# Latent attention in layer 0: where TensorE makes the queries, who copies the turned keys, and when the low parts of w_out0a are cut

## What is computed

```
z, xbc, dt_raw, q_a, kv_a, k_pe = split_cols(h @ w_in, L0_SIZES)
...
y = ssd_chunked(xs, dt, a, b, c)
y = y + d_skip * xs
y_ssd = rmsnorm(y * silu(z), ssm_norm_g)
q = rmsnorm(q_a, q_a_norm_g) @ w_q_b                 # 8 heads of 64 + 32, the 32 rotated by position
kv = rmsnorm(kv_a, kv_a_norm_g) @ w_kv_b             # 8 heads of 64 (key) + 64 (value)
k = concat(kv[..., :64], broadcast(apply_rope(k_pe)))  # 32 rotated key rows, the same for all heads
o_mla = causal_block_attention(q, k, kv[..., 64:], 96 ** -0.5)
return concat([y_ssd, o_mla]) @ w_out
```

## Time and profile before

| | us |
|---|---|
| median of 3 executions | 2051.86 |
| lowest, highest | 2048.86, 2054.71 |
| the profiled execution | 2055.55 |
| its span | 2053.8 |
| TensorE busy | 1928.1 (94%) |
| VectorE busy | 1379.4 (67%) |
| ScalarE busy | 985.5 (48%) |
| GpSimd busy | 262.5 (13%) |
| mean granted TensorE clock | 0.977 of full |

### The profile page before, as it was taken

One profiled execution on the slowest core, in us unless ns is written; L12 is line 12 of the kernel. 1 busy time (PEld: TensorE's weight loads), 2 busy tenths in 40 slices (PEclk: granted clock), 3 DMA queues, 4 the chain that ended last, 5 costly groups with the idle time before them and its releaser, 6 DMA issues.

```text
span 2053.8 us, 33496 instructions
## 1 busy us (share of the span) xinstructions
PE 1928.1 (94%) x13340; PEld 1775.8 (86%) x13340; DVE 1379.4 (67%) x2512; ACT 985.5 (48%) x1431; POOL 262.5 (13%) x121
## 2 busy tenths in 40 slices
PE   5889899998998789998999989999999999999998
PEld 5886699988987579998998889999998888999997
DVE  4897665557965755334766548988878887666665
ACT  5444454445434444445555545566653334444444
POOL 1001044440001013442000047100000000000000
PEclk9998999999999899999999999999999999999999
DMA  7653456654645235555544434477776776455452
GB/s 299 231 198 115 147 207 246 246 215 165 216 169 179 93 116 212 188 188 176 182 144 144 144 137 153 177 209 208 216 218 243 288 261 231 177 233 189 181 200 108
DMA packets 94234, 392.82 MB, mean 191 GB/s; under 512 B 7648, under 2 KB 41584, under 8 KB 55552
## 3 DMA queue, kind: packets, MB, share of 16 engines
q1 hardware_dynamic: 94080, 390.69, 54.3%
HBM read 372.83 MB, written 15.73 MB: 189 GB/s over the span
## 4 chain that ended last, share of the span: by engine, by line
PE 75%; DVE 14%; ACT 3%; issue 2%; DMA 0%; POOL 0%; DVEq 0%; ACTq 0%
PE ps L563 10%; PE ps L565 10%; PE ps L564 10%; PE acc L559 8%; PE acc L560 8%; PE acc L561 8%; DVE wlo L1272 3%; PE acc L563 3%; PE acc L564 3%; PE acc L565 3%; DVE arena L1301 2%; PE acc L1227 1%; PE ps L1227 1%; PE ps L626 1%; PE acc L1000 1%
## 5 line engine op out<-in xcount | busy, mean ns | idle before, releaser
L2284 ACT ACTIVATE whi<-raw 128x1024 fp32r<-128x1024 f32 x559 | 588.9, 1058 | 501.9 <-PE acc L561 279.0
L1272 DVE TENSOR_TENSOR wlo<-raw,whi 128x1024 fp32r<-128x1024 f32 x460 | 567.1, 1241 | 316.3 <-ACT whi L2284 315.2
L563 PE MATMUL ps<-hhi,whi 128*128 128x256 f32 x1896 | 541.7, 286 | 10.9 <-DVE wlo L1272 6.2
L564 PE MATMUL ps<-hlo,whi 128*128 128x256 f32 x1896 | 537.0, 283 | 0.0
L565 PE MATMUL ps<-hhi,wlo 128*128 128x256 f32 x1896 | 536.9, 283 | 0.0
L563 PEld LDWEIGHTS ps<-hhi,whi 128*128 128x128 f32 x1896 | 363.9, 192 | 17.8 <-ACT hhi L2396 3.7
L564 PEld LDWEIGHTS ps<-hlo,whi 128*128 128x128 f32 x1896 | 364.1, 192 | 2.9
L565 PEld LDWEIGHTS ps<-hhi,wlo 128*128 128x128 f32 x1896 | 363.9, 192 | 0.0
L1272 POOL TENSOR_TENSOR wlo<-raw,whi 128x1024 fp32r<-128x1024 f32 x99 | 245.5, 2483 | 689.6 <-ACT whi L2284 689.4
L559 PE MATMUL acc<-whi,chi 128*128 128x512 f32 x752 | 297.8, 396 | 10.0 <-DVE wlo L1272 8.4
L560 PE MATMUL acc<-whi,clo 128*128 128x512 f32 x752 | 296.0, 394 | 0.0
(11 more groups left out here) (449 smaller groups left out, 2420.3 us busy)
## 6 DMA issues: line engine op xcount, KB each, us to landing
raw<-in_peer_down SPq DMA_DIRECT2D x64, 1024.0 KB, 4.9
raw<-in_peer_up SPq DMA_DIRECT2D x64, 1024.0 KB, 5.1
arena<-in_ada SPq DMA_DIRECT2D x80, 512.0 KB, 4.9
raw<-in_w_gate SPq DMA_DIRECT2D x22, 1024.0 KB, 4.8
raw<-in_w_up SPq DMA_DIRECT2D x22, 1024.0 KB, 5.0
raw<-in_w_down SPq DMA_DIRECT2D x22, 1024.0 KB, 4.7
arena<-spill SPq DMA_DIRECT2D x14, 1024.0 KB, 6.9
spill<-hT_t SPq DMA_DIRECT2D x22, 448.0 KB, 6.5
```

Source lines behind the costliest of these rows:

```text
L563: e.matmul(out, hi, xh, start=start, stop=False, skip_group_check=True)
L564: e.matmul(out, hi, xl, start=False, stop=False, skip_group_check=True)
L1272: e.tensor_tensor(out=lo, in0=w, in1=hi.bitcast(F32), op=ALU.subtract).then_inc(*X(("lo", j)))
L2284: e.activation(hi, w, ACT.Copy, scale=1.0).then_inc(*self.A(("hi", j)))
```

## The change

1. In ssd, TensorE makes the first half of the queries before the state (as soon as `low_normed` and its banks allow) and the second half between state and y. They go to banks 0 to 3 (ACC) and stay there; state and y take ROT.
2. In mla, TensorE makes keys first, then the sums of squares, then values.
3. ScalarE copies the queries after TensorE's end of ssd, then the 32x2048 turned keys (before: VectorE), then squares y, then copies the keys, and only then takes the root of the sums (before: ahead of the keys). TensorE's scores wait for `keys_turned` as well.
4. In each softmax the cut of one block of `w_out0a` (2, then 6) moves ahead: on ScalarE before the exponentials, on VectorE between maxima and reciprocals. `ve_out_by_rows` then cuts by row tile, with the second `ve_ada` step between the second and the third of the remaining cuts instead of before them.

```diff
@@ pe_ssd
+        e.wait_ge(*self.at("low_normed"))
+        self.pe_queries(e, 0)
+        self.banks.order = ROT
         e.wait_ge(*self.at("xdd"))
         e.wait_ge(*self.at("out", "b_tok"))
         for g in range(2):
             ps = self.banks.take(e, "state", g)
...
+        self.pe_queries(e, 1)
         for i in range(0, 8, 2):
...
             t.then_inc(*self.P(("full", "y", i)))
+        self.banks.order = ALL
         self.P.mark("end", "ssd", "P")
+
+    def pe_queries(self, e, i):
+        for h0 in (4 * i, 4 * i + 2):
+            self.banks.hold(e, ACC[h0 // 2], "w_qh", h0)
+        self.pe_heads_in(e, "w_qh", i, 3, self.m.qa, 96)
@@ pe_heads_in
-            ps = self.banks.take(e, name, h0)
+            ps = self.banks.tile(name, h0) if name == "w_qh" else self.banks.take(e, name, h0)
@@ pe_mla
-        e.wait_ge(*self.at("low_normed"))
-        for i in range(2):
-            self.pe_heads_in(e, "w_qh", i, 3, m.qa, 96)
-        self.pe_rstd(e, "ssm", [range(0, 4), range(4, 8)], m.tmp, lambda j: e.wait_ge(*self.at("y_square", j // 2 * 2)))
         for i in range(2):
             self.pe_heads_in(e, "w_kh", i, 2, m.kva, 64)
+        self.pe_rstd(e, "ssm", [range(0, 4), range(4, 8)], m.tmp, lambda j: e.wait_ge(*self.at("y_square", j // 2 * 2)))
...
         e.wait_ge(*self.at("mla_rope"))
+        e.wait_ge(*self.at("keys_turned"))
         e.wait_ge(*self.at("out", "w_kvv", 1))
@@ VectorE
+    def ve_out_by_rows(self, e, name, ks):
+        for k in ks:
+            self.cut_lo(e, self.V, self.W.last(name, 2 * k + 1, 512) + 2)
+            if k % 2 == 0:
+                self.ve_ada(e)
@@ ve_mla
-        e.tensor_copy(m.kn[64:96, :, :], bc(m.kp[64:96, :].unsqueeze(1), [32, 8, T])).then_inc(*V())
...
-                           lambda hs, n: bc(m.cb0[:, 256 - nk:256].unsqueeze(1), [128, n, nk]), m.St0)
-            self.ve_out(e, "w_out0a", range(4 * qt, 4 * qt + 4))
+                           lambda hs, n: bc(m.cb0[:, 256 - nk:256].unsqueeze(1), [128, n, nk]), m.St0,
+                           ahead=self.W.last("w_out0a", 8 * qt + 1, 512) + 2)
+            self.ve_out_by_rows(e, "w_out0a", range(4 * qt, 4 * qt + 4))
@@ se_mla
         e.wait_ge(*self.at("end", "ssd", "P"))
-        e.wait_ge(*self.at("end", "ssd", "V"))
+        e.wait_ge(*self.at("mixed", 1))
...
-        self.se_rstd(e, "ssm", 2, 512, m.rs4[:, 0:2, :])
+        e.wait_ge(*self.at("kp"))
+        e.activation(m.kn[64:96, :, :], bc(m.kp[64:96, :].unsqueeze(1), [32, 8, T]), ACT.Copy, scale=1.0)
...
+        self.se_rstd(e, "ssm", 2, 512, m.rs4[:, 0:2, :])
+        e.wait_ge(*self.at("end", "ssd", "V"))
...
         for qt in range(2):
             nk = 128 * (qt + 1)
+            self.cut_hi(e, self.W.last("w_out0a", 8 * qt + 1, 512) + 2)
             self.se_scores(e, f"mla{qt}", 8, nk, m.St0)
```

More of the change, by code:

```diff
@@ L2509, in se_ssd @@
                 *A(("out", "state", g)))
-        for i in range(0, 8, 2):
-            e.wait_ge(*self.at("y", i))
-            e.activation(m.tmp[:, i:i + 2, :], m.y[:, i:i + 2, :], ACT.Square, scale=1.0).then_inc(*A(("y_square", i)))
         A.mark("end", "ssd", "A")
@@ L2523, in se_mla @@
                          scale=1.0).then_inc(*A(("out", "w_qh", h0)))
-        self.se_rstd(e, "ssm", 2, 512, m.rs4[:, 0:2, :])
+        e.wait_ge(*self.at("kp"))
+        e.activation(m.kn[64:96, :, :], bc(m.kp[64:96, :].unsqueeze(1), [32, 8, T]), ACT.Copy, scale=1.0).then_inc(
+            *A(("keys_turned",)))
+        for i in range(0, 8, 2):
+            e.wait_ge(*self.at("y", i))
+            e.activation(m.tmp[:, i:i + 2, :], m.y[:, i:i + 2, :], ACT.Square, scale=1.0).then_inc(*A(("y_square", i)))
         for h0 in range(0, 8, 2):
```

## The result

| | before | changed |
|---|---|---|
| median of 6 executions each, us | 2054.82 | 2044.21 |
| lowest, highest | 2048.86, 2056.44 | 2040.97, 2045.49 |
| the profiled execution | 2055.55 | 2044.72 |
| its span | 2053.8 | 2042.9 |
| VectorE, ScalarE, GpSimd busy | 1379.4, 985.5, 262.5 | 1378.7, 986.7, 263.4 |

The ratio is 0.9956, with a 95% interval of 0.9946 to 0.9967: faster by 6.8 to 11.1 us, where 16.5 were forecast. The time lies in the range given (2030 to 2045), near its slow end. By the medians it is 10.6 less; against the 2051.86 from which the forecast was subtracted, it is 7.7 less. The traces show why: two of the three terms of the sum came as forecast (6.2 and 5.3), the other gave 2.7 of 4.9, and a fourth, which had been set at nothing, took 4.5 back, some 900 us behind the change.

The account below looks back on a forecast made before the run. TensorE, busy for 94% of the span, was taken as the bound, with three waits and the slow-clock stretches behind them to win. Gains 4.9 + 6.2 + 5.4 = 16.5 from 2051.86 gave 2035.4 us, range 2030.0 to 2045.0.

Parts of the forecast that it names:

- part 2: First softmax: cutting block 2 early removes TensorE's 3.25 us wait and 2.9 of slow clock, gaining 6.2.
- part 3: Second softmax: cutting block 6 early leaves one wait of 2.0 for block 7, gaining 5.4 us.
- The norm of ffn0: Sign behind the second softmax: ffn0's norm should come 16 to 17 us earlier.
- The turn of the banks costs nothing in the sum: Later bank takes: changed holders cost 0, being copied out by work TensorE's next step waits for anyway.
- Slower, by the turn of the banks: Rival, chance 0.03: TensorE waits 5.12 us for changed holders at each of six places, 30.7 in all, giving 2066.1.
- a stage behind mla that is longer: Sign that the prediction is wrong: any stage after mla taking longer than before; no size given.
- Part 1: From the decays to the scores: queries around the state, turned keys on ScalarE, gaining 4.9 us.
- the bound without a wait for the banks: Upper bound at the first queries: no bank wait at 148.9, 1.6 us more, 6.5 instead of 4.9.
- Part 3's clock: Second softmax: TensorE's idle time of 2.0 us was taken to cost no clock; the other end was 2.9.
- VectorE as the bound: Rival, chance 0.20: VectorE bounds both softmaxes, its chain running 2 us late; gain about 11, time 2040.9.
- VectorE beside GpSimd: First softmax: block 2's cut delayed perhaps 0.7 us, scalings win 1.0, nothing summed; by the skill page, gain 5.7.
- behind mix1 each stage as long as before, within 1: Sign for the stages after mix1: each keeps its earlier length to within 1 us.

Follow-up runs that it names:

- run 3: The kernel before with only the changed softmax cuts of w_out0a, queries and turned keys as before: 2041.03 us, ratio 0.9944.
- run 1: The changed kernel with the turn of the banks moved on by four at mix1, restoring the old holders from there: 2039.82 us, ratio 0.9930.
- run 2: The kernel before with nothing but the turn of the banks moved on by four at mix1: 2057.55 us, ratio 1.0026.
- run 4: The base with the cuts of w_out0a as before the change, leaving the moved queries and ScalarE's turned keys: 2049.09 us, ratio 0.9977.
- run 5: The base with the turned keys copied by VectorE again instead of ScalarE: 2043.70 us, ratio 0.9947.
- run 7: The base with VectorE's adaLN steps behind the odd row tiles' low part instead of the even ones': 2039.72 us, ratio 0.9932.
- run 9: The changed kernel with the turn of the banks moved on by four only at mix2: 2040.63 us, ratio 0.9945.
- run 6: The base with the two halves of the queries swapped in their accumulator banks and ScalarE's copies reordered to match: 2038.06 us, ratio 0.9928.
- base: The changed kernel with the banks turned back at mix1, the same kernel as run 1: 2039.82 us, ratio 0.9930.
- run 10: Run 6 with each softmax's first adaLN step behind the odd row tile's low part, the second behind VectorE's turned-probabilities copy: 2033.50 us, ratio 0.9909.

## Why the prediction was right and wrong

**The sign and the mechanism near the change: right.** The state ran at full clock (1.88 for the 1.9 forecast), TensorE has no break over 1 from the first queries to the scores, and those wait for the copy of the values. There is no wait for block 3, the clock is 1.00 through the first softmax, and one wait of 1.90 for block 7 stands where 2.0 was written. Parts 2 and 3 came as 11.5 for 11.6, and run 3 shows that they are worth that by themselves. The norm of ffn0 came 14.2 earlier (243.85 for 258.07) where 16 to 17 were written.

**"The turn of the banks costs nothing in the sum": the step that failed.** Its reason was that a changed holder "was copied out by work that TensorE's next step waits for anyway". At `w_out2` that holds for the four row tiles together, not for the first: before, the first began at 1107.99, with `moba_proj` 2 only just being copied out and 3 not yet. But `pe_out` holds all four accumulator banks ahead of its first product:

```
if first:
    for b in ACC:
        self.banks.hold(e, b, nm, "acc", b)
```

Before, these held `gmlp_proj` 1, 2, 3 and `moba_proj` 0; with the turn four further, `moba_proj` 1, 2, 3 and `gmlp_proj` 0. So the first product waits for the last copy, and the first row tiles no longer lie beside VectorE's copies: 4.85 more ahead of the first product (5.95 against 1.10) and 2.1 of clock behind it (28.6 from the first product to the idle time at the memory's norm, against 28.9 less 2.4 of waits), less the 2.4 of the other two waits, 4.5. The rival "Slower, by the turn of the banks" had this mechanism, with a chance of 0.03, and spread it over six places at 5.1 each. The traces show it in one, at 4.5, and the ratios make it some 5 (0.9930 against 0.9956 in run 1, 1.0026 in run 2). It is also what the prediction named as a sign of being wrong, "a stage behind mla that is longer".

**Part 1, 4.9 forecast, 2.7 measured: a term that was mis-sized.** Two pieces. The queries started at 151.03 instead of 150.5, half of it because everything before was 0.3 later in this execution. And the first half was costed at 5.3, at full clock; it took 6.87. (The y's, 5.3 in the sum and from no row, took 5.7, from 164.72 to 170.44; steps that overlap at their edges make up for that.) The prediction weighed the clock behind 2.0 of idle time only in part 3 and took the nearest row, 1.00 behind 1.96. Ahead of the first queries there is no such row: TensorE comes out of small products and stands 1.9. In all six profiled executions that have this wait (changed kernel, runs 1, 4, 5, 7, 9) the clock was 0.50 behind it, falling by its end or up to 1.3 later, and the first queries took 6.87 (changed kernel), 7.08 (runs 1, 4 and 9), 7.95 (run 5) and 8.29 (run 7); in run 6, without the wait, 5.42. The 1.6 that the prediction named as the bound without a wait for the banks was to be had by two edited lines, and the clock with it.

**Part 3's clock: right by luck.** Behind the same wait of 1.90 in the second softmax the clock stayed at 1.00 in the changed kernel and in runs 3 and 6, and fell to 0.50 for 3.4 us in runs 1, 5 and 9. The two windows, changed kernel and base:

```profile
216.80:220.20 3.40, 3.40 (x18) 2.83 (x19) 3.26 (x4) 0.00 (x0) 0.00 (x0) 1.00 0.75 219
```

```profile
216.50:219.90 3.40, 3.40 (x9) 2.63 (x10) 3.26 (x4) 0.00 (x0) 0.00 (x0) 0.50 0.74 263
```

9 products instead of 18 in the same time. The price of such a wait is 0 or about 1.6, and one trace shows only one of the two.

**VectorE as the bound: it wasn't, by a hair.** With the keys' copy still on it the first softmax is 2.1 longer (run 5). ScalarE's 1.91 for the turned keys (2.0 forecast) cost nothing. The Trainium skill's page "ScalarE: Activation LUTs" (section "Rules for kernel authors") tells authors to use VectorE and not ScalarE for relu, max, min, add and mul; carried over to this copy it would have left it on VectorE. The rows speak against that here, since ScalarE's 0.7 more lies beside TensorE's keys and VectorE's 1.22 doesn't.

**VectorE beside GpSimd: right, and larger elsewhere.** The cut of block 2 took 1.78 for 1.22, 0.6 more where "one GpSimd instruction, 0.7" was allowed for; four scalings took 1.65, the next four 0.87. In run 5, where GpSimd was done before them, the cut took 1.22 and the same four scalings 0.87. What the text missed is the normalizing ahead of them, 3.25 before, 3.73 after and 5.71 in run 5. By the Trainium skill's page "SBUF — State Buffer" (section "Who interferes with whom") a VectorE instruction with two SBUF inputs contends with GpSimd's reads; cut and normalizing are such, and the rows agree. That block 3 would come late by it, and part 2 be 5.7, did not come: there was slack.

**The rest, +1.2: two stretches with opposite signs.** The second part of gated linear attention with the head of the attention behind it, between the same two waits, takes 74.6 before (584.63 to 659.24) and 72.4 after (571.73 to 644.10), 2.2 less. From the second turning to its start it is 350.8 before and 352.1 after, 1.3 more, and 0.9 of that is in mix1, from the wait of 4.49 to that of 0.69 (493.84 to 508.59 before, 480.07 to 495.69 after). So "behind mix1 each stage as long as before, within 1" failed in two stages, here and at `w_out2`. In both the half clock lasts differently long; in mix1 it is some 3 us before and over 6 after. In the later one the kernel before has two stretches at half clock, from about 586 to 589 and this one:

```profile
595.90:602.70 6.80, 6.80 (x25) 4.42 (x25) 1.17 (x4) 2.69 (x4) 0.00 (x0) 0.50 0.64 231
```

The changed kernel lacks the first and has half of the second (from about 584 to 587.5). Run 1, with the changed kernel's code but for the turn, has both again (74.6, from 570.55 to 645.13); run 3, with the turn of before, has what the changed kernel has (72.3). So they can go without a change of holders. But the three traces with the changed holders (changed kernel, runs 2 and 9) take 72.4, 70.7 and 72.3, and of the nine with the old ones eight take 73.0 or more: whether the holders have a part in it isn't shown, and stays open.

## What to carry to other kernels

Where a program hands out banks or buffers by a counter, any take that is added or removed shifts every later owner: list the owners before and after, and look first at places that claim several at once ahead of their first use, for these wait for the slowest. An edit that only moves work should keep the counter (one line, worth 4.5 us here by the traces). When a wait is shortened by moving a piece of VectorE's work, put what is left behind the last thing that somebody waits for, not merely behind the thing that was late: run 7 gave back most of what it won, run 10 kept it.

## What the runs showed of the hardware

- An idle time of TensorE has no fixed price. The same wait of 1.9 was followed by clock 0.50 in 3 of 6 profiled executions in one place and in 6 of 6 in another, and the same wait of 3.25 by more than 6 us of it before and 3.4 in run 4. A single wait's clock cost is therefore known from one trace only as one of its values.
- That the four executions of run 3 fell in two pairs (2036.9 and 2037.0, 2045.1 and 2045.2), and those of the kernel before lay between 2043.5 and 2056.5, would fit stretches at half clock that come and go; only the profiled ones show it, so of the others it is argued and not shown. The prediction had allowed for executions up to 3 from the median; 2043.5 is 8.6 below its own.
- VectorE's instructions with two SBUF inputs were up to 1.8 times as long beside GpSimd's (5.71 against 3.25 for eight, 1.78 against 1.22 for one), and four scalings 1.9 times (1.65 against 0.87).
